# Two transformer blocks on one core: dense products of the mixers as three single-pass matmuls, norms block by block, first mixer reordered

## The reference

```
first_block (16 meta tokens in front: T = 272):
  n    = rmsnorm(h);  proj = n @ w_in
  y_gdn = gated delta rule of conv/silu(q,k,v), chunked; rmsnorm; * silu(gz)
  y_dsa = attention of aq,ak,av over the 64 keys that an index score (iq,ik,iw) selects
  merged = sigmoid(gate_a) * (y_gdn @ w_branch_gdn) + sigmoid(gate_b) * (y_dsa @ w_branch_dsa)
  h = h + rmsnorm(merged @ w_out)
  h = h + rmsnorm(square(relu(rmsnorm(h) @ w_up)) @ w_down)
second_block (a context of 256 tokens, scale and shift by w_mod):
  q,k,v,f,gate2a,gate2f = modulate(rmsnorm(x)) @ w_in;  k,v of the context too
  heads = differential attention;  four = 2-D Fourier transform of f
  y = sigmoid(gate2a) * (heads @ w_ao) + sigmoid(gate2f) * (four @ w_fo);  x = x + g1 * (y @ w_o)
  x = x + g2 * (16 experts, 2 of one group of 4 for each token);  result = rmsnorm(x)
```

## Time and profile before

| | |
|---|---|
| time, median of 3 runs | 1523.97 us (1523.35 to 1549.17) |
| profiled execution: time, span | 1523.4 us, 1521.3 us |
| busy: PE, PEld, DVE, ACT, POOL | 91%, 74%, 36%, 23%, 8% |
| mean granted TensorE clock | 0.954 |
| DMA | 260.79 MB, mean 171 GB/s |

### The profile page before, as it was taken

How to read it: one execution, slowest core, us unless ns; L and a number is a source line. 1 busy time by engine, 2 the same in 40 slices (tenths; PEclk the granted TensorE clock), 3 DMA queues, 4 the chain that set the end, 5 groups by cost and what they waited for, 6 DMA issues and landing times.

```text
span 1521.3 us, 19937 instructions
## 1 busy us (share of the span) xinstructions
PE 1391.8 (91%) x8366; PEld 1124.6 (74%) x8366; DVE 544.4 (36%) x1044; ACT 354.3 (23%) x631; POOL 126.2 (8%) x74
## 2 busy tenths in 40 slices
PE   5996899989999994999996999998899889999995
PEld 4884799967787883999994747865788656666663
DVE  2688654152524105575324011167201241111112
ACT  1165422220205012454331000056000111101001
POOL 0000142000000000445430000000000000000000
PEclk8997899999999997999997999999999989999998
DMA  8335100223240454445454222200343689999970
GB/s 316 139 130 202 56 2 1 82 85 127 83 150 33 162 194 166 160 175 193 167 176 158 109 83 80 86 29 0 139 186 143 262 356 420 420 421 421 420 296 28
DMA packets 36005, 260.79 MB, mean 171 GB/s; under 512 B 4016, under 2 KB 4160, under 8 KB 4560
## 3 DMA queue, kind: packets, MB, share of 16 engines
q1 hardware_dynamic: 35136, 255.66, 43.0%
q0 software_dynamic: 784, 3.88, 0.6%
HBM read 258.48 MB, written 1.05 MB: 171 GB/s over the span
## 4 chain that ended last, share of the span: by engine, by line
PE 83%; DVE 12%; ACT 3%; issue 2%; DMA 0%; POOL 0%; DVEq 0%; SPq 0%; ACTq 0%
PE bank L481 51%; PE bank L1006 12%; PE bank L823 6%; PE bank L1023 2%; PE bank L621 2%; PE bank L606 2%; PE bank L616 1%; DVE q L1836 1%; DVE attn L1645 1%; DVE rB L1456 1%; PE bank L518 1%; DVE prod L1488 1%; DVE stat L1818 1%; DVE qc L1504 1%; PE bank L881 1%
## 5 line engine op out<-in xcount | busy, mean ns | idle before, releaser
L481 PE MATMUL bank<-nT,ring 128*128 128x256 f32 (+1 forms) x992 | 227.0, 389 | 7.2 <-DVE nT L1462 7.2
L481 PEld LDWEIGHTS bank<-nT,ring 128*128 128x128 f32 x992 | 190.9, 193 | 42.8 <-DVE nT L1462 7.7
L481 PE MATMUL bank<-hcl,ring 128*128 128x256 f32 (+1 forms) x576 | 158.2, 435 | 6.0 <-DVE hcl L1796 6.0
L481 PEld LDWEIGHTS bank<-hcl,ring 128*128 128x128 f32 x576 | 112.0, 195 | 50.2 <-issue 31.1
L481 PE MATMUL bank<-nMs,mlp_parts 128*128 128x256 f32 x768 | 95.0, 288 | 11.3 <-DVE mlp_parts L1750 11.3
L481 PEld LDWEIGHTS bank<-nMs,mlp_parts 128*128 128x128 f32 x768 | 94.7, 197 | 11.8 <-issue 11.8
L1124 POOL TENSOR_TENSOR mlp_parts<-ring,mlp_parts 128x512 fp32r<-128x512 f32 x32 | 88.7, 2771 | 157.1 <-ACT mlp_parts L1314 157.1
L823 PE MATMUL bank<-up,mlp_parts 128*128 128x256 f32 x768 | 92.7, 283 | 0.0
L823 PEld LDWEIGHTS bank<-up,mlp_parts 128*128 128x128 f32 x768 | 92.4, 192 | 0.1
L1750 DVE TENSOR_TENSOR mlp_parts<-ring,mlp_parts 128x1536 fp32r<-128x1536 f32 x32 | 56.2, 1757 | 87.9 <-ACT mlp_parts L1314 87.8
L1314 ACT ACTIVATE mlp_parts<-ring 128x2048 fp32r<-128x2048 f32 x32 | 61.1, 1912 | 107.9 <-PE bank L481 58.4
(11 more groups left out here) (426 smaller groups left out, 1933.0 us busy)
## 6 DMA issues: line engine op xcount, KB each, us to landing
ring<-stream SPq DMA_DIRECT2D x174, 1024.0 KB, 4.9
more<-stream SPq DMA_DIRECT2D x66, 1024.0 KB, 15.0
c<-constants_one SPq DMA_DIRECT2D x1, 1653.0 KB, 17.6
qc<-h_in SPq DMA_DIRECT2D x1, 1088.0 KB, 5.1
c<-constants_two POOLq DMA_DIRECT2D x1, 1056.0 KB, 7.8
hT<-h_in POOLq DMA_DIRECT2D x1, 1024.0 KB, 17.1
ctxT<-ctx_in POOLq DMA_DIRECT2D x1, 1024.0 KB, 5.8
result<-h2tok SPq DMA_DIRECT2D x1, 1024.0 KB, 3.9
```

The lines of the kernel that those rows point to most:

```text
L481: last = nc.tensor.matmul(dst, lhs, rhs, start=(i == 0), stop=(i == len(pairs) - 1))
```

## The change

- 63 units of both mixers get the MLP's form: `gz aq ak iq gate_a bg gate_b bd wo` (31) and `q2 k2 v2 f2 gate2a ao gate2f fo wo2` (32). With the 32 of the MLP they are numbered through in `SPLIT`. `gk gv gq av ik iw`, `mod`, attention and the experts stay in float32.
- The split is made in one way everywhere: ScalarE copies the unit into one of two buffers `w_high` (`highs`), VectorE subtracts all 2048 columns and writes the low part over the unit in the ring (`lows`, `ring_low`). GpSimd takes no part. The calls `after_unit` in each engine's order prepare up to two units ahead. `split_tiles` multiplies the high part first (both activation parts), then waits for the low part.
- The activations that feed these units get a high and a low part too: `nT` (in the middle of the inverses), `y_gdn`, `y_dsa`, `merged`, `hcl`, `heads`, `four`, `merged2`.
- `ik`, `iw` and `av` move from between `aq` and the index scores to behind `mod` 5, in front of the decay's small products. `gate_a` 0 moves in front of the index scores, `gate_b` 0 behind the first two logits of the attention. `choose` is cut into halves with `lows` between. The units of `gate2f` come two at a time in front of `fo`. The norm of `y_gdn` takes Ln and Exp on ScalarE in place of a root and a reciprocal of VectorE, and `aq` is drained without waiting for `y_gdn`.
- Norms go block by block: `add_blocks` sums blocks as they are squared (six of eight within the last unit of `wo`, `down` and `wo2`), the gain is applied while the bank is drained (`square_and_scale`), `add_to_stream` scales and adds each block, and the next unit waits for single blocks. At four places a dummy operation (`warm`) asks for ScalarE's root table ahead.
- The input comes in four transfers, and the residual copy `hT` is loaded after the first norm. `scattered` is signalled by bank, and the result leaves in four transfers.
- The context's part of `hcl` and the lambda are computed during `down`.

```diff
-    order += [("mod", u) for u in range(8)]
-    order += [("gz", u) for u in range(4)] + [("aq", u) for u in range(4)] + [("ak", 0), ("av", 0)]
+    order += [("mod", u) for u in range(6)] + [("av", 0)] + [("mod", u) for u in range(6, 8)]
+    order += [("gz", u) for u in range(4)] + [("aq", u) for u in range(4)] + [("ak", 0)]
...
+def stream_order(used):
+    order = list(used)
+    for units, before in (((("up", 0), ("up", 1)), ("mod", 11)), ((("q2", 0), ("q2", 1)), ("mod", 16))):
+        for unit in units:
+            order.remove(unit)
+            order.insert(order.index(before), unit)
+    return order
+USED = weight_order()
+ORDER = stream_order(USED)
+SPLIT_KINDS = ("gz", "aq", "ak", "iq", "gate_a", "bg", "gate_b", "bd", "wo", "up", "down", "q2", "k2", "v2", "f2", "gate2a", "ao", "gate2f", "fo", "wo2")
+SPLIT_UNITS = [unit for unit in USED if unit[0] in SPLIT_KINDS]
+SPLIT = {unit: d for d, unit in enumerate(SPLIT_UNITS)}
...
+            ring_low = sbr(same, "ring_low", 128, SLOTS, KT * UNIT_COLS)
...
+        w_high = sbr(dense, "w_high", 128, 2, KT * UNIT_COLS)
...
+        def prepared_after(d):
+            return min(d + 3, len(SPLIT_UNITS))
...
+            def split_unit(kind, u, cols=UNIT_COLS):
+                s, cnt = unit(kind, u)
+                d = SPLIT[(kind, u)]
+                pe.wait_ge(high_ready, d + 1)
+                return s, cnt, d, [w.rearrange("p (k n) -> p k n", n=cols) for w in (w_high[:, d % 2, :], ring_low[:, s, :])]
...
+            def low_parts(d):
+                pe.wait_ge(low_ready, d + 1)
...
+            def split_tiles(kind, u, high_x, low_x, n, names, k_ready=lambda k: None, halfway=lambda: None, drains=1):
+                s, cnt, d, (high_w, low_w) = split_unit(kind, u)
+                dst = [take(name, drains) for name in names]
...
+                for k in range(KT):
+                    k_ready(k)
                     for j in range(2):
-                        dst = take(names[j], drains)
-                        last = group(dst[:, 0:n], [(w[:, k, j * 128:(j + 1) * 128], rhs[:, k, :]) for k in range(kt)])
-                        if j == 0:
-                            done(names[0], last)
-                else:
-                    dst = take(names[0], drains)
-                    for j in range(2):
-                        last = group(dst[:, j * n:(j + 1) * n], [(w[:, k, j * 128:(j + 1) * 128], rhs[:, k, :]) for k in range(kt)])
+                        w = high_w[:, k, j * 128:(j + 1) * 128]
+                        first = k == 0 and (j == 0 or len(names) == 2)
+                        nc.tensor.matmul(into[j], w, high_x(k), start=first, stop=False, skip_group_check=True)
+                        nc.tensor.matmul(into[j], w, low_x(k), start=False, stop=False, skip_group_check=True)
+                halfway()
+                low_parts(d)
+                for j in range(2):
+                    for k in range(KT):
+                        last = nc.tensor.matmul(into[j], low_w[:, k, j * 128:(j + 1) * 128], high_x(k), start=False, stop=(k == KT - 1), skip_group_check=True)
...
+            def add_blocks(name, src, n, blocks, ready):
+                if blocks[0] == 0:
+                    take(name)
+                for k in blocks:
+                    pe.wait_ge(*ready(k))
+                    last = nc.tensor.matmul(psum[banks.at[name]][:, 0:n], ones, src[:, k, :], start=(k == 0), stop=(k == KT - 1), skip_group_check=True)
+                if blocks[-1] == KT - 1:
+                    done(name, last)
...
+            wik = ws[:, WS["ik"][0]:WS["ik"][0] + KT * 128].rearrange("p (k n) -> p k n", n=128)
+            wiw = ws[:, WS["iw"][0]:WS["iw"][0] + KT * 8].rearrange("p (k n) -> p k n", n=8)
+            dst = take("ik")
+            done("ik", group(dst[:, 0:T], [(wik[:, k, :], nT[:, k, :]) for k in range(KT)]))
+            dst = take("iw")
+            for qt in range(2):
+                a = META + qt * 128
+                last = group(dst[:, qt * 8:(qt + 1) * 8], [(nT[:, k, a:a + 128], wiw[:, k, :]) for k in range(KT)])
+            done("iw", last)
+            s, cnt = unit("av", 0)
...
-            pe.wait_ge(sq_ready, 15)
-            feature_sum("ss_mix", sq, SEQ)
+                split_tiles("wo", u, whole(merged_high), whole(merged_low), SEQ, [("wo", u)],
+                            lambda k: pe.wait_ge(merged_ready, k // 2 + 1) if u == 0 else None,
+                            lambda: add_blocks("ss_mix", sq, SEQ, range(6), lambda k: (mix_sq, k // 2 + 1)) if u == 3 else None)
+            add_blocks("ss_mix", sq, SEQ, range(6, KT), lambda k: (mix_sq, 4))
             for u in range(8, 11):
                 mod_unit(u)
-            pe.wait_ge(sq_ready, 16)
-            feature_sum("ss_h1", sq, SEQ)
+            add_blocks("ss_h1", sq, SEQ, range(KT), lambda k: (h_sq, k + 1))
...
-            for m in range(MLP_UNITS):
-                pool.wait_ge(mlp_high_ready, m + 1)
-                a = KT * UNIT_COLS - G_COLS
-                nc.gpsimd.tensor_tensor(mlp_parts[:, m % 2, 1, a:], ring[:, (MLP_FIRST + m) % SLOTS, a:],
-                                        mlp_parts[:, m % 2, 0, a:], sub).then_inc(mlp_low_ready_g, 1)
...
+            def highs(end):
+                for d in range(highs_done[0], end):
+                    s, n = split_place(d)
+                    act.wait_ge(unit_loaded[s], 16 * n)
+                    if d >= 2:
+                        split_used(act, d - 2)
+                    A(w_high[:, d % 2, :], ring[:, s, :], ACT.Copy).then_inc(high_ready, 1)
+                    highs_done[0] = d + 1
+            def after_unit(kind, u):
+                highs(prepared_after(SPLIT[(kind, u)]))
...
+            def lows(end):
+                for d in range(lows_done[0], end):
+                    dve.wait_ge(high_ready, d + 1)
+                    s, _n = split_place(d)
+                    TT(ring_low[:, s, :], ring[:, s, :], w_high[:, d % 2, :], sub).then_inc(low_ready, 1)
+                    lows_done[0] = d + 1
...
+            A(warm[:, :], eps, ACT.Sqrt)
+            for i in range(4):
+                act.wait_ge(h_loaded[i], 16)
+                A(vc[:, 2 * i:2 * i + 2, :], qc[:, 2 * i:2 * i + 2, :], ACT.Square).then_inc(in_sq, 1)
+            rms_root("ss_in", T, root[:, :])
...
+            for qt in range(2):
+                choose(qt, 0, 4)
+                after_unit("gate_a", qt)
+                choose(qt, 4, 8)
+                merge_a(qt)
+                after_unit("bg", qt)
+            for u in range(2, 4):
+                after_unit("gate_a", u)
+                merge_a(u)
+                if u == 2:
+                    after_unit("bg", u)
...
+            def add_to_stream():
+                def scale_block(k):
+                    step(TT(mix[:, k, :], mix[:, k, :], rB[:, 0:SEQ], mul))
+                    return step.n
+                scaled_at = scale_block(0)
+                for k in range(KT):
+                    following = scale_block(k + 1) if k + 1 < KT else None
+                    dve.wait_ge(dve_step, scaled_at)
+                    TT(hT[:, k, :], hT[:, k, :], mix[:, k, :], add).then_inc(h_ready, 1)
+                    scaled_at = following
...
-            scaled(nM, hT, small("g_pre_mlp"), SEQ)
-            step.settle()
-            step(CP(nMs[:, :, 0, :], nM[:, :, :]))
-            step.settle()
-            TT(nMs[:, :, 1, :], nM[:, :, :], nMs[:, :, 0, :], sub).then_inc(nM_ready, 1)
+            gains = small("g_pre_mlp")
+            for k in range(KT + 1):
+                if k < KT:
+                    STT(nM[:, k, :], hT[:, k, :], gains[:, k:k + 1], rB[:, 0:SEQ], mul, mul).then_inc(norm_ready, 1)
+                if k:
+                    dve.wait_ge(norm_high_ready, k)
+                    TT(nMs[:, k - 1, 1, :], nM[:, k - 1, :], nMs[:, k - 1, 0, :], sub).then_inc(nM_ready, 1)
...
+                dve.wait_ge(scattered, k // 2 + 1)
+                STT(hT[:, k, :], psum[4 + k // 2][:, (k % 2) * SEQ:(k % 2 + 1) * SEQ], modT[:, 40 + k, 0:1], hT[:, k, :], mul, add).then_inc(h_ready, 1)
             inv_rms("ss_out", SEQ)
-            scaled(mix2, hT, small("g_final"), SEQ, out_ready)
+            for k in range(KT):
+                STT(mix2[:, k, :], hT[:, k, :], small("g_final")[:, k:k + 1], rB[:, 0:SEQ], mul, mul).then_inc(out_ready, 1)
...
```

879 lines of the change are left out of this document (528 added, 351 removed).

## The result

The changed kernel takes 1372.55 us (median of four runs, 1365.21 to 1390.97) where the kernel before, beside it, takes 1523.66: a ratio of 0.8994, 95% interval 0.8945 to 0.9042. Forecast were 1381, range 1358 to 1416. The run at 1390.97 (clock 0.955, the others 0.963 to 0.971) and one of the four before, at 1549.17, are of a slower state and left out of the ratio. The profiled execution took 1370.9 us with a span of 1369.1, 152.2 us less than the span before.

The account below looks back on a forecast made before the run. TensorE, busy 91% of the span, was taken as the bound. Gains of 85 + 9 + 16 + 7 + 19 + 5 + 11 = 152 us less costs of 10 gave 142, so 1523.4 - 142 = 1381.4; range 1358 to 1416.

Parts of the forecast that it names:

- Products: Mixer units, `v2` and `k2` in single passes, three for four: 85 us gained (82 to 87).
- rival 1: Weight preparation on ScalarE and VectorE becomes the bound in the mixers, 63 us come back: 1444; chance 0.11.
- Start: Input in quarters and block-wise first products bring the first product to 13.7 to 15 us: gain 9 (6 to 10).
- Fill: `av`, `ik`, `iw` go into TensorE's 10.5 us wait for the decay: gain 16 (10.5 to 18).
- `y_gdn` and `aq`: TensorE's waits of 3.1 and 4.3 us there go, by early square and `aq` drain without reciprocals: gain 7.
- Norms: Norms behind `wo` and `down` go block by block: 11 and 8, together 19 us gained (12 to 24).
- Norm behind `wo2`: Block-wise norm ahead of the experts, which take over the shift in full: gain 5 (2 to 8).
- End: Block-wise work behind the last scatter, early table load and a quarter transfer: gain 11 (8 to 12).
- Attention 2: Copy and subtraction for `ao` 0 stand between `f2` and the first softmax: cost 4 (0 to 6).
- Rival 3: Gaps only move: removed waits return where the next engine is late, half of 67 us lost: 1415; chance 0.14.
- Rival 2: A mixer unit takes three quarters of the old, 5.18 us, 38 us more gained: 1343; chance 0.07.
- rival 4: Slower than before: look-ahead collapses, copy, subtraction and unit run in series: 1646; chance 0.02.

Follow-up runs that it names:

- run 5: Three pads in the local memory shift operand addresses of the changed kernel, no instruction changed: 1365.8 us against 1370.9.
- run 9: Changed kernel with the `up` units' passes of high weights with the low operand streaming 128 columns in place of 256: 1375.9 us against 1370.9.
- run 3: Changed kernel with the 31 units of the first mixer multiplied by fp32 matmuls again (high parts alone): 1403.7 us, 32.8 more.
- run 12: The changed kernel itself, unedited, timed again beside a best version: 1376.5 us (1371.1 to 1376.9), ratio to the kernel before 0.9028.
- run 4: Changed kernel with the product of high weights with the low operand left out in every unit: 1212.3 us against 1370.9.
- Run 1: Changed kernel with the `av`, `ik`, `iw` products and their evictions moved from ahead of the decay stage to behind it: 1395.2 us against 1370.9.
- Run 2: Changed kernel with TensorE's side of the norms as whole tensors: sums and first units behind wait for the last block: 1382.5 us against 1370.9.
- run 6: Changed kernel with the first seventeen transfers of expert weights issued in order of use: 1371.6 us against 1370.9.
- runs 7 and 10: Changed kernel (1370.9), exp table loaded early, low part of `ao` 0 moved: to GpSimd, 1365.2 us; to quarters on VectorE, heads 10 to 13, 1376.1 us.

## Why the prediction was right

**Products, 85 forecast (82 to 87), 87 measured.** Of the 55 units, 37 read `nT`, `y_dsa` or `hcl` and take 5.63 to 5.66 us, gaining 1.26, and 18 take 5.76, gaining 1.15: 67 for 62. The unit price was sized on MLP rows, whose operand addresses happen to be the dearer ones (run 5). `v2` came as computed, 11.3 to 11.7 us for 13.8: 9. `k2` is where I chose the wrong end: I let the load vanish under 512 columns, 217 ns a pass, and it was 229, the upper bound that I had named. Also, the 13.90 us that I started from end with a drain; from start to start the old unit took 13.73, and the new one takes 11.0: 11 for 14. The reason given for the price, a load of its own for each pass, was borne out by run 9, and the mixers' gain by run 3. The Trainium skill's rule of N / 2.4 + 2.5 ns ("TensorE: Matmul & The Clock Gate", "Wait — 56ns, not 53.3ns?") would have 109 ns for these passes; no 256-column group here went below 113.

**Preparation hidden, rival 1 rejected.** TensorE waited 3.2 us for low parts, all among the gates, and not once for a high part. The waits of 0.3, 0.4, 0.7 and 1.8 us grew from unit to unit as forecast (0.4, 0.9, 1.0 and 2.4). Idle time is not their whole cost: behind the longest the clock fell to 1.2 GHz, and the 16 passes with low weights took 213 ns each for 120. In all, the four units concerned took 5.7 us more than their price, for 5 forecast. In the repeat of run 12 the same wait left the clock at 1.00, and the stretch is 1.5 us shorter (77.3 for 78.8). Attention 1, put at a cost of 1, gained 1.4 instead, with `gate_b` 0 in its first wait. How narrow it was elsewhere shows run 4: in `aq` VectorE had 6.7 us of work for a unit of 6.5. The estimate of 6.9 against 6.6 was sound, and the verdict "0" rested on the look-ahead alone.

**Start, 9 forecast, 8.7 measured**; first `gk` product at 14.60.

**Fill, 16 forecast (10.5 to 18), 15.5 measured by the table: right, but by favour of the clock.** The wait of 10.5 us was filled. In the profiled execution the rest of the work came nearly free, as argued, because the stretch stayed at the higher clock (from the first `mod` unit to the first mask: clock 0.78 before, 0.95 after). From that `mod` unit to `gz` the kernel before took 148.3 us and the changed one 152.2 with 18.1 us of work more: 14.2 of the 15.5 lie there, the rest ahead of it. The five other executions that took 157.3 to 157.4 gained only 9.1, less than the 10.5 that I had set as the lower bound for a clock that gives nothing. So the size of this term depends on the execution, and 5 us of the profiled 1371 can be luck; the repeat, with a median of 1376.5, still lies in the range. Run 1 brings the wait back, but at a price of 4 to 9 us and not of 16.

**`y_gdn` and `aq`, 7 forecast, 10 measured** (43.6 less 18.1 moved and 15.2 of units).

**Norms, 19 forecast (12 to 24), 25.8 measured**, above its own upper bound: the term that was furthest off, and the one that most explains why the profiled execution took 1371 and not 1381. Behind `wo` 14.6 for 11, behind `down` 11.2 for 8. Run 2 puts 17 of it on TensorE's side. What I had mis-sized is what remains in series: I let `up` 0 and `q2` 0 run behind VectorE at 0.9 us a block, and they waited only 2.0 and 2.2 us.

**Norm behind `wo2`, 5 forecast, 1 measured**: a step that failed. I wrote that TensorE, not DMA, has the work there. Experts' weights come in a burst of 17 MB at some 420 GB/s once `wo2` is done, and the first unit in use stood twelfth. In the kernel before it landed in time; with the path some 11 us shorter TensorE waited 3.6 for it, and the experts ran 3 us longer. With the order mended (run 6) the term is 6. The sum of six blocks inside `wo2`'s last unit, part of this very change, puts the burst off by 2.4 us more (run 2). That the first pass reads the unit that stands twelfth, I could have seen in the order of the transfers.

**End, 11 forecast, 9.9 measured. Attention 2, 4 forecast, 3.1 measured**; runs 7 and 10 confirm that place, and that it can't be had back cheaply. **`heads`, 0 forecast, 2 lost** (6.9 us of waits for 5.0).

Rival 3 did not come about as a whole: of the waits removed, only the one ahead of the experts came back in part, and run 1 shows that 5 us of the fill can be had behind the decay stage too (148.3 and 18.1 us of work for 161.5). Rival 2 is ruled out by the passes' price, rival 4 by the 3.2 us of waits for low parts.

## What to carry to other kernels

Price a split product by its weight loads: three passes for four gave 16 to 18%, not 25; with 512 columns to a load (`k2`) it was 20%. Before handing extra work to an engine, add up its whole list for the stretch in which it lands; here the averages (51% busy) hid one stretch at its limit. When a path gets shorter by some microseconds, look at the order in which transfers for the stage behind it are issued, and at what their issue waits for. And before a gain is put down to an edit, see how the same instructions ran in the other executions on record: here one stretch without an edit varied by 7 us.
